# Second blocks: the decay gate's 8 columns ride on the latent input, the latent input stands second, and the hand-written order of the side steps is changed with it

## The reference

```python
h = rmsnorm(x, norm_w); proj = h @ w_in          # 3752 columns, split into:
# m_cq 256, m_ckv 128, m_kr 32, m_gate 256, g_q 512, g_k 512, g_v 512, g_z 512, g_b 4, g_a 4,
# c_q 256, c_k 256, c_v 256, c_gate 256
y_mla  = mla_mixer(m_cq, m_ckv, m_kr, ...) * silu(m_gate)
y_gdn  = gdn_mixer(g_q, g_k, g_v, g_z, g_b, g_a, ...)
y_moba = moba_mixer(c_q, c_k, c_v, t5_table) * silu(c_gate)
x = x + concat([y_mla, y_gdn, y_moba]) @ w_out

# gdn_mixer
q, k, v = silu(causal_conv(concat([q, k, v]), conv_w))       # 4 taps
q, k = l2norm(q) * 128 ** -0.5, l2norm(k)
beta = sigmoid(b); g = -exp(A_log) * softplus(a + dt_bias)    # b, a: the 8 gate columns
gc = cumsum(g) per chunk; decay = exp(gc_t - gc_j), lower triangle
L = strict(beta * (k k^T) * decay); solve (L + I) [W, U0] = [k.., v..]; A = (q k^T) * decay
# then a chunk-wise recurrence of W, U0, A; rmsnorm of the result; * silu(z)

# mla_mixer: latent attention
q = rmsnorm(c_q) @ w_uq; kv = rmsnorm(c_kv) @ w_ukv; rope; causal softmax attention, 4 heads
```

## Time and profile before

| | |
|---|---|
| median of 3 runs | 1312.41 us (1312.31 to 1314.3) |
| profiled execution | 1312.83 us, span of its trace 1311.0 us |
| PE busy | 1288.7 us of the span, 98% |
| DVE, ACT, POOL busy | 1033.3, 726.5, 50.2 us |
| second layer 0 | its first input ends at 979.2 us, its last products at about 1136 us |
| second layer 1 | its first input ends at 1148.9 us |

### The profile page before, as it was taken

One profiled execution on the slowest core, in us unless ns is written; L12 is line 12 of the kernel. 1 busy time (PEld: TensorE's weight loads), 2 busy tenths in 40 slices (PEclk: granted clock), 3 DMA queues, 4 the chain that ended last, 5 costly groups with the idle time before them and its releaser, 6 DMA issues.

```text
span 1311.0 us, 26108 instructions
## 1 busy us (share of the span) xinstructions
PE 1288.7 (98%) x10692; PEld 1228.1 (94%) x10692; DVE 1033.3 (79%) x1715; ACT 726.5 (55%) x1084; POOL 50.2 (4%) x48
## 2 busy tenths in 40 slices
PE   8999999999999999999999999999999999999997
PEld 8899999999999999999999999999998999889996
DVE  7999998677876777999997778776777756777565
ACT  6554566556544555544657555544567546566364
POOL 0000000000000000100000000000000110001100
PEclk9999999999999999999999999999999999999999
DMA  8555554565565466655355556555554324343232
GB/s 297 193 193 193 161 161 163 192 214 187 203 205 204 145 209 217 219 168 193 120 202 175 192 180 229 194 201 204 174 181 164 99 71 148 117 159 114 82 101 77
DMA packets 109711, 226.23 MB, mean 173 GB/s; under 512 B 6260, under 2 KB 17780, under 8 KB 109592
## 3 DMA queue, kind: packets, MB, share of 16 engines
q1 hardware_dynamic: 104656, 218.91, 49.6%
q10 hardware_dynamic: 4936, 5.65, 1.3%
HBM read 223.49 MB, written 1.06 MB: 171 GB/s over the span
## 4 chain that ended last, share of the span: by engine, by line
PE 81%; DVE 11%; ACT 4%; issue 2%; DMA 1%; POOL 0%; SPq 0%; ACTq 0%; POOLq 0%; DVEq 0%
PE bank L536 29%; PE bank L545 15%; PE bank L558 11%; PE bank L510 8%; PE bank L566 6%; DVE wlo L1904 4%; PE bank L597 3%; PE bank L515 2%; PE bank L625 2%; PE bank L647 2%; DVE w L2113 2%; PE bank L604 2%; ACT whi L1265 1%; DMA ring<-in_w_in 1%; DVE w L2457 1%
## 5 line engine op out<-in xcount | busy, mean ns | idle before, releaser
L1904 DVE TENSOR_TENSOR wlo<-ring,whi 128x1024 fp32r<-128x1024 f32 (+3 forms) x428 | 498.2, 1190 | 156.6 <-ACT whi L1265 135.4
L1265 ACT ACTIVATE whi<-ring 128x1024 fp32r<-128x1024 f32 (+3 forms) x428 | 431.3, 1024 | 321.6 <-PE bank L536 192.3
L536 PE MATMUL bank<-hboth,whi 128*128 128x256 f32 x3648 | 449.7, 276 | 0.0
L536 PEld LDWEIGHTS bank<-hboth,whi 128*128 128x128 f32 x3648 | 428.0, 192 | 1.8 <-issue 0.3
L545 PE MATMUL bank<-hboth,wlo 128*128 128x256 f32 x1824 | 247.4, 277 | 0.0
L545 PEld LDWEIGHTS bank<-hboth,wlo 128*128 128x128 f32 x1824 | 223.3, 192 | 3.8 <-issue 3.2
L558 PE MATMUL bank<-whi,hboth 128*128 128x512 f32 (+2 forms) x448 | 98.8, 363 | 0.0
L2113 DVE SCALAR_TENSOR_TENSOR w<-w,par 128x256 f32<-128x256 f32 x240 | 98.0, 477 | 0.0
L510 PE MATMUL bank<-w 64*64 64x64 f32 (+6 forms) x1312 | 89.7, 247 | 6.0 <-ACT w L1619 4.3
L558 PEld LDWEIGHTS bank<-whi,hboth 128*128 128x128 f32 x448 | 80.3, 189 | 9.3 <-issue 0.9
L510 PEld LDWEIGHTS bank<-w 64*64 64x64 f32 (+3 forms) x1312 | 75.2, 150 | 14.0 <-ACT w L1619 4.7
(11 more groups left out here) (312 smaller groups left out, 1532.3 us busy)
## 6 DMA issues: line engine op xcount, KB each, us to landing
ring<-in_w_in SPq DMA_DIRECT2D x100, 1024.0 KB, 5.1
ring<-in_w_ffn_down SPq DMA_DIRECT2D x22, 1024.0 KB, 5.1
ring<-in_w_ffn_gate SPq DMA_DIRECT2D x20, 1024.0 KB, 5.2
ring<-in_w_ffn_up SPq DMA_DIRECT2D x20, 1024.0 KB, 5.1
ring<-in_w_merge SPq DMA_DIRECT2D x8, 1024.0 KB, 5.1
ring<-in_w_out SPq DMA_DIRECT2D x8, 1024.0 KB, 4.9
ring<-in_w_oc SPq DMA_DIRECT2D x4, 1024.0 KB, 5.0
ring<-in_w_od SPq DMA_DIRECT2D x4, 1024.0 KB, 5.0
```

Source lines behind the costliest of these rows:

```text
L536: done = e.matmul(o, wh[:, k, cols(u)], paired(s_[:, k0 + k, :]), stop=False, skip_group_check=True, start=opens and k == 0 and s_ is sh a ...
L1265: e.activation(part_of(whi, j), part_raw(j), ACT.Copy).then_inc(*up("hi.a"))
L1904: e.tensor_tensor(part_of(wlo, j), part_raw(j), part_of(whi, j), ALU.subtract).then_inc(*up("lo.v"))
```

## The change

- The gate's 8 columns are moved in the weight (on the host) behind the latent input's 416, which gets 424 columns (m0). The tile `wba`, its load, its split, its 24 matmuls, the copy of 8 rows and the turns back are gone; `b` stands in columns 416 to 423 of the copied latent input, and DVE reads `a` from the bank (`t4a`).
- m0 is the second input, ahead of qc, and takes two "s" banks instead of "m" banks.
- The taps of the keys' second half are two steps (places 8 and 9), one for each block of channels; their Silu is at place 10.
- `decay` is at places 14 to 19 instead of 8 to 11; the keys' squares are at place 13 and their sums at 16, the key scores at 25, the factors at 27, `BT` at 31, and the levels of the solve, with `M6` at 52, `MT6` at 53, `U` and `W` at 54.
- `latent` steps 0 to 3 are at 18, 21, 22 and 25 instead of 24, 27, 28 and 32; `later_rows` is behind part 5, now of m0.
- `Mm` (the copy of `M`) has a buffer of its own, which no longer is that of `Dm`; ACT's first copy therefore needs no wait for the scores `A`.

```diff
-TWO_IN = (("kc", 1184, 1696), ("qc", 672, 1184), ("m0", 0, 416), ("vc", 1696, 2208),
-          ("cqk", 2728, 3240), ("cvg", 3240, 3752), ("mg", 416, 672), ("z", 2208, 2720))
+TWO_IN = (("kc", 1192, 1704), ("m0", 0, 424), ("qc", 680, 1192), ("vc", 1704, 2216),
+          ("cqk", 2728, 3240), ("cvg", 3240, 3752), ("mg", 424, 680), ("z", 2216, 2728))
 TWO_PLAN = {
-        "ba": [4, 7, 7],
-        "others": [26, 32, 39, 39, 51],
-        "decay": [8, 8, 10, 11],
-        "taps": [12, 18, 32],
-        "delta": [15, 16, 18, 18, 28, 28, 34, 35, 37, 39, 41, 44, 44, 46, 46, 48, 49, 50, 51, 52, 53, 60, 63, 64, 64],
-        "latent": [24, 27, 28, 32, 34, 35, 37, 41, 44, 51, 52, 63, 64],
+        "decay": [14, 15, 17, 19],
+        "taps": [8, 9, 10, 26, 26, 26, 32, 32, 32],
+        "others": [30, 39, 43, 45, 51],
+        "delta": [13, 16, 25, 27, 31, 31, 37, 38, 40, 42, 44, 46, 47, 48, 49, 51, 52, 53, 54, 55, 56, 60, 63, 64, 64],
+        "latent": [18, 21, 22, 25, 34, 35, 37, 41, 44, 51, 52, 63, 64],
         "softmax": [37, 39, 52, 54],
...
-        bg = st[:, 128:144].rearrange("p (t n) -> p t n", t=2)
+        bg = xn[:, :, 416:424]
...
             def delta_p(l):
-                yield 0
-                e.wait_ge(*at("kc", l))
-                for tb in range(2):
-                    scores_p("delta.p", l, tb, kc, "L")
                 yield 1
                 squares_p("delta.p", l, ksq, "kc")
+                yield 2
+                e.wait_ge(*at("kc", l))
+                for tb in range(2):
+                    scores_p("delta.p", l, tb, kc, "L")
...
-                        held = Held(*(lambda i=i: ps.take(e, "m", name, l, i) for i in range(2)))
+                        held = Held(*(lambda i=i: ps.take(e, "s" if name == "m0" else "m", name, l, i) for i in range(2)))
...
-                    else:
-                        e.wait_ge(*at("A", l, 1))
                     e.activation(Mm[r], by64(bank("M", l, lv))[r], ACT.Copy).then_inc(*up("delta.a"))
...
-                        if name == "qc" and i == 1:
+                        if name == "m0" and i == 1:
                             later_rows(l)
...
-                            e.activation(m0[:, tb], bank(name, l, tb)[:, 0:416], ACT.Copy).then_inc(*up("two.a"))
+                            e.activation(xn[:, tb, 0:424], bank(name, l, tb)[:, 0:424], ACT.Copy).then_inc(*up("two.a"))
...
                 for i in range(3):
-                    yield i
-                    four_taps(l, i, 1)
+                    if i == 0:
+                        for u in range(2):
+                            yield u
+                            four_taps(l, i, 1, (u,))
+                    else:
+                        yield 3 * i
+                        four_taps(l, i, 1)
...
-                e.wait_ge(*at("bg", l))
-                e.tensor_copy(bg, blocks(bank("bg", l)[:, 0:16])).then_inc(*up(name))
...
+                e.wait_ge(*at("m0", "done", l))
+                for tb in range(2):
+                    e.tensor_tensor(t4a[:, tb], bank("m0", l, tb)[:, 420:424], prm("dtb", l), ALU.add).then_inc(*up(name))
+                    leave(name, "m0", l, tb)
```

More of the change, by code:

```diff
@@ L177 @@
         "decay.p", "decay.a", "decay.v", "latent.p", "latent.a", "latent.v", "latent.g",
-        "outs.a", "outs.v", "ba.p", "ba.a", "ba.v", "others.p", "others.a", "others.v", "others.g", "delta.p", "delta.a", "delta.v", "delta.g")
-DMAS = ("x0", "x1", "id", "c", "p", "p0", "pos", "tab", "gn", "sc", "bi", "fl", "u", "rg", "ba", "fn", "out")
+        "outs.a", "outs.v", "others.p", "others.a", "others.v", "others.g", "delta.p", "delta.a", "delta.v", "delta.g")
+DMAS = ("x0", "x1", "id", "c", "p", "p0", "pos", "tab", "gn", "sc", "bi", "fl", "u", "rg", "fn", "out")
 def build(nc, a, out):
@@ L207, in build @@
         st = sb("st", [P, 320])
-        wba = sb("wba", [P, 64])
-        bhi = sb("bhi", [P, 64], F32R)
-        blo = sb("blo", [P, 64], F32R)
         sgb = sb("sgb", [P, 4, S])
@@ L311, in build @@
         wukv = bufC[:, 0:512]
-        gs = xn[:, :, 736:992].rearrange("p t (a d) -> p t a d", a=2)
-        rows8 = part2(23040, S)[0:8]
+        gs = xn[:, :, 744:1000].rearrange("p t (a d) -> p t a d", a=2)
         m0 = xn[:, :, 0:416]
-        mtmp = xn[:, :, 416:1024]
+        mtmp = xn[:, :, 424:1024]
         qm = [heads(b[:, 0:384]) for b in (bufA, bufB)]
@@ L339, in build @@
         T_, LTc, TTc, Mm = (by64(b) for b in (big[:, 20 * S:22 * S], big[:, 26 * S:28 * S], bufI[:, 0:512],
-                                              bufH[:, 0:512]))
+                                              big[:, 4 * S:6 * S]))
         BT, LTx = (by64(b) for b in halves(flat(yT[:, 2:6])))
@@ L901, in bias_p @@
                     put("bias.p", "bias", i)
[L903 to L913, removed]
-            def decay_p(l):
-                yield 0
-                bk = ps.take(e, "s", "bg", l)
-                e.wait_ge(*at("rows8", l))
-                for tb in range(2):
-                    done = turn(bk[:, 8 * tb:8 * tb + 8], rows8[:, cols(tb)])
-                done.then_inc(*up("decay.p"))
-                put("decay.p", "bg", l)
+            def decay_p(l):
                 yield 2
@@ L1057, in delta_p @@
             def delta_p(l):
-                yield 0
+                yield 1
+                squares_p("delta.p", l, ksq, "kc")
+                yield 2
                 e.wait_ge(*at("kc", l))
@@ L1061, in delta_p @@
                     scores_p("delta.p", l, tb, kc, "L")
-                yield 1
-                squares_p("delta.p", l, ksq, "kc")
                 yield 4
@@ L1175, in two_p @@
                 j = two0(l)
-                side = Tasks(ba=ba_p(l), others=others_p(l), decay=decay_p(l), delta=delta_p(l), latent=latent_p(l))
+                side = Tasks(others=others_p(l), decay=decay_p(l), delta=delta_p(l), latent=latent_p(l))
                 def between(j):
@@ L1195, in two_p @@
                     else:
-                        held = Held(*(lambda i=i: ps.take(e, "m", name, l, i) for i in range(2)))
+                        held = Held(*(lambda i=i: ps.take(e, "s" if name == "m0" else "m", name, l, i) for i in range(2)))
                         for i in range(4):
                             if name == "m0":
-                                toks(j, held, 416, hh, 2 * i, i == 0, i == 3, between(j))
+                                toks(j, held, 424, hh, 2 * i, i == 0, i == 3, between(j))
                             else:
@@ L1571, in ffn_a @@
                     bias_rows()
-                    load_ba(0)
                 j = ffn0(l)
@@ L1614, in taps_a @@
                 for i, tag in enumerate(("kc", "qc", "vc")):
-                    yield i
+                    yield 3 * i + 2
                     for p_ in range(2):
@@ L1644, in decay_a @@
                 yield 2
+                e.wait_ge(*at("m0", "in", l, 1))
                 e.activation(ebn, bg[:, :, 0:4], ACT.Exp, scale=-1.0).then_inc(*up("decay.a"))
@@ L1725, in delta_a @@
             def delta_a(l):
-                yield 1
+                yield 0
                 squares_a("delta.a", l, kc, ksq, "kc")
@@ L1777, in two_a @@
                 j = two0(l)
-                side = Tasks(ba=ba_a(l), taps=taps_a(l), others=others_a(l), decay=decay_a(l), delta=delta_a(l), latent=latent_a(l),
+                side = Tasks(taps=taps_a(l), others=others_a(l), decay=decay_a(l), delta=delta_a(l), latent=latent_a(l),
                              outs=outs_a(l))
@@ L1851, in two_a @@
                         put("two.a", "mgs", l)
-                if l == 0:
-                    e.wait_ge(*at("ba", "lo", l))
-                    load_ba(1)
                 if l == L - 1:
@@ L2446, in bias_v, with four_taps @@
                     leave("bias.v", "bias", i)
-            def four_taps(l, i, p_):
+            def four_taps(l, i, p_, blocks_=(0, 1)):
                 tag, dst, c0 = (("kc", kc, 4), ("qc", qc, 0), ("vc", vc, 8))[i]
@@ L2452, in four_taps @@
                 for k4 in range(3):
-                    for u in range(2):
+                    for u in blocks_:
                         c = 2 * p_ + u
@@ L2600, in delta_v @@
                 name = "delta.v"
[L2601 to L2604, removed]
                 yield 1
@@ L2609, in delta_v @@
                 put(name, "kss", l)
-                e.wait_ge(*now(name))
+                yield 2
+                for tb in range(2):
+                    e.wait_ge(*at("Dm", l, tb))
+                    scores_v(name, l, tb, "L", LT, Dm)
+                yield 3
                 e.wait_ge(*at("edl", l))
@@ L2615, in delta_v @@
                 e.reciprocal(pk, pk).then_inc(*up(name))
-                yield 2
                 e.wait_ge(*now(name))
@@ L2739, in two_v @@
                 j = two0(l)
-                side = Tasks(ba=ba_v(l), taps=taps_v(l), others=others_v(l), decay=decay_v(l), delta=delta_v(l), latent=latent_v(l),
```

(5 more changed lines are left out.)

## The result

| | before | after |
|---|---|---|
| median | 1312.75 us (5 runs, 1312.31 to 1314.3) | 1341.7 us (5 runs, 1341.46 to 1342.87) |
| span of the profiled execution, mean granted clock | 1311.0 us, 0.997 | 1339.7 us, 0.984 |
| layer 0, from the end of the keys' products to the next layer's first product | 979.2 to 1136.2: 157.0 us | 978.8 to 1149.1: 170.3 us |
| layer 1, from the end of the keys' products to PE's last two matmuls | 1148.7 to 1303.7: 155.0 us | 1161.6 to 1332.4: 170.7 us |

The ratio is 1.0223, with a 95% interval of 1.0212 to 1.0234: the changed kernel is slower by 29 us. All of it lies in the two second layers, 13.4 and 15.7 us.

A forecast was written before the change was run, and what follows sets the result against it. TensorE, busy 98%, was taken as the bound. New waits of 18.3 us a layer, less the gate's 2.5 and old waits, gave +10.9 and +11.9, together +22.8 on 1312.8: 1335 us (forecast 1322 to 1339, range 1312 to 1348).

The forecast's parts named there:

- The four late places: New PE waits per layer: latent products (place 22) 8.0 us, `BT` (31) 3.0, logits (35) 2.9, `U` and `W` (54) 4.4.
- The gate: Second layers: 24 gate matmuls removed from PE, 2.62 us, less 0.16 for added columns; net 2.5 us a layer, 5.0 in all.
- I take 0: Half-clock stretches behind the new waits, up to 1.7 us each, counted as no loss; bound up to 3.5 us a layer.
- The lead holds: Rival: ACT and DVE stay ahead of PE, place 22 ready by 1001.8; about 1303 us; chance 0.17 together with "Only the gate".
- Only the gate: Rival: only the gate changes, no chain moves, -5.0 us to 1308; chance 0.17 together with "The lead holds".
- Only the front is late: Rival: waits up to place 22 come, solve and place 54 catch up; +2.2, about 1315 us; chance 0.20.
- All waits and the clock: Rival: each long wait drops the clock and little is absorbed; +22.8 + 7, 1342 us; chance 0.13.
- The rule on table switches: ACT: about 2.7 us per table switch would put place 22 2.8 us later a layer, sum 5.7 higher; trace's 1.28 used.
- One table more in each layer: ACT: keys' Silu ahead of softplus and exponentials, queries' Silu behind them, so one extra table load per layer, 1.28 us.

The follow-up runs named there:

- its best version: Changed kernel with the solve at its old places, latent step 2 at place 24, taps joined, keys' squares' sums at 19: 1319.62 us, ratio 1.0056.

## Why the prediction was right, and which term was short

- **Direction, place and mechanism held.** The steps were ready when the hand-written queues said, within 1.1 us: squares' sums at 991.8 (forecast 992.5), latent products 1008.8 (1009.8), `BT` 1031.5 (1032.6), logits 1044.6 (1044.8), `U` and `W` with 1.1 + 3.65 us of waiting on the last half-part (4.4).
- **The four late places** were sized as 8.0 + 3.0 + 2.9 + 4.4 = 18.3 us a layer at full clock. The trace has 12.6 us of waits in layer 0, and the rest as slow matmuls ahead of the next ready time; so single waits came out shorter than forecast, 1.5 instead of some 4 us at the latent copies, 0.9 instead of 2.9 at the logits. The run with PE kept busy shows the exchange: nearly the same start times, with longer waits. There 9.5 us of waits and 8.3 us of filling matmuls (2.40, 2.17 and 3.74) make 17.8 us, against 18.3.
- **The gate** as an amount of PE time (2.5 us a layer) is right, but it was not a gain of its own: its end goes into the wait at place 16, as the sum had it by taking that wait to an absolute time. The run that left most of it out shows the same on the kernel before.
- **The mis-sized term is the clock, "I take 0".** The sum was +22.8, measured +28.9; 1341.7 us lies 2.7 us above the 1339 that ended the forecast's own band, inside the wider range. Behind place 54 no ACT or DVE step sets a later time; 3.75 - 2.05 = 1.7 us are lost on the first 16 matmuls there and some more on those after them, 2.4 us in layer 0, where the miss is 13.4 - 10.9 = 2.5. Layer 1 misses 15.7 - 11.9 = 3.8. There the stretch behind place 54 loses 1.6 us (9.2 us from `U` and `W` at 1286.42 to the matmuls at 1295.64, 7.6 with PE kept busy). Its logits also start later, 66.7 us after the keys' products instead of layer 0's 65.8, after a wait of 2.2 us, and from there to `U` and `W` it takes 58.1 instead of 56.5 us:

```profile
1228.31 1.51 PE L505 MATMUL bank<-w 96*128 96x128 f32 x8 [2.21 <-ACT w L1662]
1229.47 3.40 PE L531 MATMUL bank<-hboth,whi 128*128 128x256 f32 x16
```

  In layer 0 the same 16 matmuls take 2.03 us. The waits at places 53 and 54 are as long in layer 1 as in layer 0 (1.1 and 3.65 us), so what was lost behind the logits was not taken out of them. The run with PE kept busy has these slow matmuls too (3.22 us), so no run prices this part by itself. The prediction had the bound (3.5 us a layer) and the reason for absorption, but did not ask at which of the waits absorption ends.
- **The rivals.** "The lead holds" fell: it needed place 22 ready by 1001.8, and it was ready at 1008.8. "Only the gate" fell with it, and its 5.0 us for the gate were not to be had even on the kernel before. "Only the front is late" fell by the two runs on the solve, whose places cost 14.4 us alone and 19.6 us with the front. "All waits and the clock", 1342, is nearest in number, which is luck: its reason, that little is absorbed, is wrong behind two of the three waits that were filled.
- **The rule on table switches.** The Trainium skill, "ScalarE: Activation LUTs", "Rules for kernel authors", would have added 5.7 us to the sum by about 2.7 us a switch. The loads here take 1.28 us, and the copies at place 22 came 1 us earlier than forecast with that number, so the excess doesn't come from the tables there. "One table more in each layer" holds for layer 0 alone (8 loads, 7 before); layer 1 has 7 and 7, since the keys' Silu finds its table loaded there.

**What stays open.** With the solve in its old places the changed kernel is still 9.4 us slower than before, and 7.0 in its best version. Putting the latent steps back at their old places, or `Dm` at 23, made it worse, since the queries' Silu (place 26, before 18) and copies now stand in their way; a table that has the old front with only the gate merged, which would price the merging by itself, was not run. Nor does any run show why three of the four executions with PE kept busy gained so little (1340.11 to 1341.37 us).

## What to carry to other kernels

In a kernel whose engines run fixed queues, a step has the time of whatever stands ahead of it in its own queue: before moving it, name the instruction that it will stand behind and what that one waits for. Four moves here (the latent steps, `Dm`, `BT`, the keys' squares) were meant to relieve a wait and made a kernel slower by 8 to 15 us, each time since a step that PE needs came to stand behind a Silu, a tap or a copy. Count time saved on the busiest engine only as far as the next wait that another engine sets, and count slow matmuls only where no such wait follows. Moving a step later doesn't have to relieve it: the copy of 0.7 us for `U` and `W`, moved with them by three places, came to stand behind the logits' maxima and a split, and PE waited 3.6 us for it.

## What was not expected of the hardware

- The granted clock doesn't follow the length of the last wait alone. After 2.48 us without work in layer 0 it fell in the changed kernel (0.50 in the window above) and not in the kernel with the solve's old places, whose 16 matmuls at 991.29 take 1.97 us and lie in this window:

```profile
991.30:993.00 1.70, 1.70 (x16) 1.70 (x16) 1.13 (x4) 1.68 (x3) 0.00 (x0) 1.00 0.94 301
```

  In the same two kernels `BT` waits 2.29 us; its 32 matmuls take 1.98 us in the one and 1.15 in the other. In layer 1 of the second kernel the keys' squares wait 2.34 us, and there its clock does fall (0.52 from 1168 to 1172). What decides between them wasn't found.
- A busy share tells nothing of speed: PE is busy for 97% in a kernel that is 29 us longer, 12 us of which it counts as busy.
